# A hybrid decoder step: the sample's gated attention laid out by head and token, and rotary tables multiplied by their norm weights once per row

## The reference

```
A    = (q * exp(b)) (k * exp(-b))^T, kept where s <= t and the sample is the same
o    = (q * exp(b)) S + A v
S'   = exp(b_last) * S + (k * exp(b_last - b))^T v
out  = rms_norm(o) * weight * silu(r)
```

## Time and profile before

| | us |
|---|---|
| median of 3 runs | 5138.36 (5134.91 to 5141.19) |
| the profiled execution | 5144.09 |
| its span, first to last instruction | 5142.4 |
| granted TensorE clock, mean | 0.931 |
| stage of the sample's gated attention | 1398.3 to 1500.5 |
| stage of the prompt's attention | 1708.5 to about 2009 |

### The profile page before, as it was taken

The page is one execution under the profiler, slowest core; times in us unless marked ns, Lnnn a source line. Parts: engine busy times, 40 slices in busy tenths (PEclk is TensorE's granted clock), DMA queues, the critical chain, the costliest instruction groups (busy, mean ns, idle before and its releaser), DMA issues.

```text
span 5142.4 us, 56147 instructions
## 1 busy us (share of the span) xinstructions
PE 4326.8 (84%) x18857; PEld 2636.9 (51%) x18857; DVE 2540.6 (49%) x5464; ACT 1773.5 (34%) x4656; POOL 1531.9 (30%) x1445
## 2 busy tenths in 40 slices
PE   6999999985458467897988989889888898888997
PEld 5888888873345455343434434334444343443361
DVE  3111111126532494224666666666666666666645
ACT  3111111114302354212444444444444444444433
POOL 0000000004420591001443444444434444444423
PEclk9999999996659778898999999999999999999979
DMA  8798989762226674316999999999999999999979
GB/s 266 265 320 295 325 289 305 264 220 88 86 91 246 208 227 161 132 54 245 421 420 421 407 421 411 412 421 409 421 414 411 421 412 418 418 407 418 410 292 386
DMA packets 312463, 1626.90 MB, mean 316 GB/s; under 512 B 43176, under 2 KB 86280, under 8 KB 170296
## 3 DMA queue, kind: packets, MB, share of 16 engines
q0 software_dynamic: 164032, 1166.28, 55.4%
q1 hardware_dynamic: 112752, 236.06, 13.5%
q10 hardware_dynamic: 35456, 221.91, 13.0%
HBM read 1541.75 MB, written 311.61 MB: 360 GB/s over the span
## 4 chain that ended last, share of the span: by engine, by line
DMA 29%; PE 17%; ACT 4%; issue 3%; POOL 1%; DVE 0%; DVEq 0%; POOLq 0%; SPq 0%; ACTq 0%; PEldq 0%
DMA ex_rows<-scratch_uv,ex_E 29%; PE ex_ps_y L2451 13%; PE ex_ps_q L2420 3%; PE ex_ps_t L2383 1%; ACT ex_diag L2176 1%; ACT ex_w L2168 1%; POOL ex_rows L2113 1%; ACT L2164 1%; ACT L2159 1%; ACT ex_gel L2164 0%; ACT L2135 0%; ACT L2133 0%; PE ex_ps_s L2433 0%; DVE ex_dots L2317 0%; ACT ex_ex L2159 0%
## 5 line engine op out<-in xcount | busy, mean ns | idle before, releaser
L2451 PE MATMUL ex_ps_y<-ex_rows,ex_diag 128*128 128x512 f32 (+1 forms) x4224 | 2019.7, 613 | 315.8 <-ACT ex_diag L2176 293.9
L2317 DVE CUSTOM_DVE_ANT_0 ex_rows<-ex_rows,ex_n2u 128x1024 f32<-128x1024 f32 x1056 | 1294.6, 1226 | 943.6 <-DMA ex_rows<-scratch_uv,ex_E 925.2
L2113 POOL DMA_INDIRECT ex_rows<-scratch_uv,ex_E x1056 | 1135.8, 1076 | 1732.0 <-PE ex_ps_y L2451 1538.9
L2451 PEld LDWEIGHTS ex_ps_y<-ex_rows,ex_diag 128*128 128x128 f32 (+1 forms) x4224 | 747.4, 189 | 1479.8 <-ACT ex_diag L2176 747.3
L344 PE MATMUL pj_ps<-pj_w_hi,pj_nT 128*128 128x470 f32 x3072 | 699.3, 378 | 23.6 <-PE pj_ps L350 12.3
L2164 ACT ACTIVATE ex_gel<-ex_dots 128x1 f32<-128x1 f32 x1056 | 214.0, 203 | 1362.3 <-DVE ex_dots L2317 1361.2
L344 PEld LDWEIGHTS pj_ps<-pj_w_hi,pj_nT 128*128 128x128 f32 x3072 | 580.1, 189 | 109.1 <-issue 29.4
L2176 ACT ACTIVATE ex_diag<-ex_ident,ex_w 128x128 f32<-128x128 f32 x1024 | 411.1, 401 | 33.6
L248 DVE COPY pj_zo<-pj_ps 128x470 f32<-128x470 f32 x96 | 61.4, 646 | 725.9 <-PE pj_ps L344 502.8
L344 PE MATMUL pj_ps<-pj_w_lo,pj_nT 128*128 128x470 f32 x1536 | 361.5, 377 | 0.0
L248 ACT COPY pj_zo<-pj_ps 128x470 f32<-128x470 f32 x96 | 51.9, 552 | 830.1 <-PE pj_ps L344 469.3
(11 more groups left out here) (361 smaller groups left out, 3797.6 us busy)
## 6 DMA issues: line engine op xcount, KB each, us to landing
pj_w<-in_w_in POOLq DMA_DIRECT2D x24, 1880.0 KB, 34.3
scratch_z<-pj_zo SPq DMA_DIRECT2D x192, 235.0 KB, 11.1
scratch_uv<-in_peer_u ACTq DMA_DIRECT2D x8, 4096.0 KB, 25.8
scratch_uv<-in_peer_v ACTq DMA_DIRECT2D x8, 4096.0 KB, 43.2
scratch_uv<-in_peer_u ACTq DMA_DIRECT2D x4, 8192.0 KB, 42.5
scratch_uv<-in_peer_v ACTq DMA_DIRECT2D x4, 8192.0 KB, 73.3
out_dk_s<-in_cache_dil_k ACTq DMA_DIRECT2D x8, 4088.0 KB, 43.8
out_dv_s<-in_cache_dil_v ACTq DMA_DIRECT2D x8, 4088.0 KB, 55.9
```

The lines of the kernel that those rows point to most:

```text
L2113: pool.indirect_dma_start(out=rows[:, p % SLOTS, :], out_offset=None, in_=d["uv"], in_offset=bass.IndirectOffsetOnAxis(ap=E[:, turn % 4, k ...
L2317: nc.vector.tensor_tensor_reduce(out=row, in0=row, in1=n2u[:, tile % 2], scale=1.0, scalar=0.0, op0=ALU.mult, op1=ALU.add, accum_out=dots[ ...
L2451: last = nc.tensor.matmul(y[0:n, 512 * c:512 * c + 512], diag[:, p % DIAGS, 0:n], rows[:, p % SLOTS, D + 512 * c:D + 512 * c + 512], start ...
```

## The change

In `gla_sample`, head and token together (4 x 32) now stand on the partitions: `q`, `k`, `v`, `r` are loaded head by head into 32 partitions each. The output is made upright: for each sample and head one product with `own_q` (`qin` with the columns of all other samples zero) as weights and the state's 256 columns moving, the four heads into four quarters of the partitions of one bank. Added states use the quarter of the partitions that belongs to the head, and a bank per head. New states go into a second tensor `S2` and are stored one by one as they are made. `og` is stored from ScalarE's queue. `er` (the gate) gets the norm weight on GpSimd. At the end of the stage's programs SyncE loads the prompt's whole rotary table, and GpSimd multiplies it by the norm weights, 8 products, and stores the result (1024 rows x 2 KB) into the scratch tensor `n2`.

In `attend`, that result is loaded per turn (2 KB a row, two buffers) in place of the table (1 KB a row); the table product and the six broadcasts of weights are gone. The load for turn u waits for `t1` and `t2` of turn u-2.

```diff
 @block.sync   # gla_sample
-            sp.dma_start(qk[:], z[rows, C_Q:C_Q + 2 * H * DK].rearrange("t (h e) -> t h e", e=DK)).then_inc(z_in, 16)
...
+            for h in range(H):
+                sp.dma_start(q[heads[h]], z[rows, C_Q + h * DK:C_Q + (h + 1) * DK]).then_inc(qk_in, 16)
+                sp.dma_start(k[heads[h]], z[rows, C_K + h * DK:C_K + (h + 1) * DK]).then_inc(qk_in, 16)
+            for h in range(H):
+                sp.dma_start(v[heads[h]], z[rows, C_V + h * DV:C_V + (h + 1) * DV]).then_inc(v_in, 16)
+            for i in range(B):
+                sp.dma_start(S[:, i], d["state_gla"][i].rearrange("h p e -> p h e")).then_inc(S_in, 16)
+            sp.dma_start(tab[:], d["rope"][0:SEQ, :].rearrange("(n p) (c e) -> p n c e", p=P, c=2)).then_inc(tab_in, 16)
+            for n, g in enumerate((d["dil_qn_g"], d["dil_kn_g"])):
+                sp.dma_start(gain[:, 0, n, :], g.partition_broadcast(P)).then_inc(tab_in, 16)
...
-            sp.wait_ge(og_done, 1)
-            sp.dma_start(d["acts"][rows, 0:H * DV], og[:]).then_inc(stored, 16)
-            for q in range(B):
-                sp.wait_ge(S_done, q + 1)
-                sp.dma_start(d["gla_state_s"][q].rearrange("h p e -> p h e"), S[:, q]).then_inc(stored, 16)
+            for i in range(B):
+                sp.wait_ge(S_done, H * (i + 1))
+                sp.dma_start(d["gla_state_s"][i].rearrange("h p e -> p h e"), S2[:, i]).then_inc(stored, 16)
 @block.gpsimd
+            for h in range(H):
+                pool.dma_start(own_causal[heads[h]], d["own_causal"]).then_inc(consts_in, 16)
+                pool.dma_start(own[heads[h]], d["own"]).then_inc(consts_in, 16)
...
+            nc.gpsimd.tensor_tensor(er[:], er[:], gn[:], ALU.mult).then_inc(scaled, 1)
+            pool.wait_ge(tab_in, 16 * 7)
+            for n in range(NT):
+                nc.gpsimd.tensor_tensor(tg[:, n], tab[:, n].unsqueeze(2).to_broadcast([P, 2, 2, DK]), gain[:], ALU.mult).then_inc(tg_done, 1)
+            pool.wait_ge(tg_done, NT)
+            pool.dma_start(d["n2"][0:SEQ, 0:512].rearrange("(n p) x -> p n x", p=P), tg[:].rearrange("p n c q e -> p n (c q e)")).then_inc(tg_stored, 16)
+            pool.wait_ge(tg_stored, 16)
 @block.vector
+            for i in range(B):
+                own_tokens = slice(T * i, T * i + T)
+                last = nc.vector.tensor_copy(own_q[:, i, :, own_tokens], qin[:, :, own_tokens])
+            last.then_inc(ownq_done, 1)
...
+            nc.vector.tensor_tensor(own_k[:], kinT[:].unsqueeze(1).to_broadcast([P, B, DK]), own[:].unsqueeze(2).to_broadcast([P, B, DK]),
+                                    ALU.mult).then_inc(ownk_done, 1)
+            def new_state(i):
                 for h in range(H):
+                    dve.wait_ge(kv_done, H * i + h + 1)
+                    nc.vector.scalar_tensor_tensor(out=S2[:, i, h, :], in0=S[:, i, h, :], scalar=eb[:, h, T * i + T - 1:T * i + T],
+                                                   in1=ps_kv[:, h, 0:DV], op0=ALU.mult, op1=ALU.add).then_inc(S_done, 1)
+            dve.wait_ge(S_in, 16 * B)
+            for i in range(4):
+                new_state(i)
+            dve.wait_ge(rms_done, 1)
+            dve.wait_ge(scaled, 1)
+            nc.vector.scalar_tensor_tensor(out=og[:], in0=o_v, scalar=stat[:, 2:3], in1=er[:], op0=ALU.mult, op1=ALU.mult).then_inc(og_done, 1)
+            for i in range(4, B):
+                new_state(i)
 @block.tensor
+            def added_state(i):
+                for h in range(H):
+                    if i:
+                        pe.wait_ge(S_done, H * (i - 1) + h + 1)
+                    nc.tensor.matmul(ps_kv[:, h, 0:DV], own_k[heads[h], i, :], v[heads[h], :], start=True, stop=True).then_inc(kv_done, 1)
+            pe.wait_ge(ownk_done, 1)
+            added_state(0)
+            pe.wait_ge(A_done, 1)
+            pe.wait_ge(ownq_done, 1)
+            pe.wait_ge(S_in, 16 * B)
             for h in range(H):
+                nc.tensor.matmul(o_v[heads[h]], A[heads[h], :], v[heads[h], :], start=True, stop=False)
+            for i in range(B):
                 for h in range(H):
+                    last = nc.tensor.matmul(o_v[heads[h]], own_q[:, i, h, :], S[:, i, h, :], start=False, stop=(i == B - 1))
+            last.then_inc(o_done, 1)
+            for i in range(1, B):
+                added_state(i)
 @block.sync   # attend, load_x
                 if is_dil(u):
-                    after(sp, tg_done, u - 2)
-                    for p0, n, a in rows(d["rope"][0:SEQ, :], u):
-                        sp.dma_start(tab[p0:p0 + n, u % 2], a.rearrange("t (c e) -> t c e", c=2)).then_inc(tab_in[u % 2].sem, 16)
+                    after(sp, t1_done, u - 2)
+                    after(sp, t2_done, u - 2)
+                    for p0, n, a in rows(d["n2"][0:SEQ, 0:512], u):
+                        sp.dma_start(tg[p0:p0 + n, u % 2], a.rearrange("t (c q e) -> t c q e", c=2, q=2)).then_inc(tg_in[u % 2].sem, 16)
 @block.gpsimd
-            def angles(u):
-                after(pool, tab_in[u % 2], u)
-                after(pool, t1_done, u - 1)
-                after(pool, t2_done, u - 1)
-                nc.gpsimd.tensor_tensor(tg[:], tab[:, u % 2].unsqueeze(2).to_broadcast([P, 2, 2, P]), gain[:],
-                                        ALU.mult).then_inc(tg_done.sem, 1)
```

More of the change, by code:

```diff
@@ L837, in _ @@
[L837 to L844 removed]
+            sp.dma_start(a[:], z[rows, C_A:C_A + RANK]).then_inc(a_in, 16)
@@ L846, in _ @@
+            sp.wait_ge(stored, 16 * B)
         @block.gpsimd
         def _(pool):
[L848 to L851, removed]
+            pool.dma_start(ident[:], d["ident"]).then_inc(consts_in, 16)
+            pool.dma_start(wg2[:], d["gla_wg2"]).then_inc(consts_in, 16)
@@ L893, in _ @@
             nc.scalar.activation(er[:], er[:], ACT.Exp, scale=-1.0).then_inc(sig_done, 1)
[L894 to L899, removed]
-            for h in range(H):
[L901 to L906, removed]
+            act.wait_ge(o_done, 1)
+            act.wait_ge(set_up, 2)
+            nc.scalar.activation(sq[:], o_v, ACT.Square, accum_out=stat[:, 0:1]).then_inc(sq_done, 1)
+            act.wait_ge(sq_done, 1)
+            nc.scalar.activation(stat[:, 1:2], stat[:, 0:1], ACT.Ln, bias=eps[:], scale=1.0 / DV).then_inc(lnv_done, 1)
+            act.wait_ge(lnv_done, 1)
+            nc.scalar.activation(stat[:, 2:3], stat[:, 1:2], ACT.Exp, scale=-0.5).then_inc(rms_done, 1)
+            act.wait_ge(og_done, 1)
+            for h in range(H):
+                act.dma_start(d["acts"][rows, h * DV:(h + 1) * DV], og[heads[h]]).then_inc(v_in, 16)
+            act.wait_ge(v_in, 16 * (3 * H + 1))
         @block.vector
@@ L932, in _ @@
             dve.wait_ge(kinT_out, 1)
-            for q in range(B):
-                nc.vector.tensor_scalar(own_k[:, q], kinT[:], own[:, q:q + 1], None, ALU.mult).then_inc(ownk_done, 1)
-            dve.wait_ge(oT_done, 1)
-            for q in range(B):
-                dve.wait_ge(kv_done, q + 1)
-                for h in range(H):
-                    last = nc.vector.scalar_tensor_tensor(out=S[:, q, h, :], in0=S[:, q, h, :],
-                                                          scalar=eb[:, h, T * q + T - 1:T * q + T],
-                                                          in1=ps_kv[:, q % 2, h, :], op0=ALU.mult, op1=ALU.add)
-                last.then_inc(S_done, 1)
+            nc.vector.tensor_tensor(own_k[:], kinT[:].unsqueeze(1).to_broadcast([P, B, DK]), own[:].unsqueeze(2).to_broadcast([P, B, DK]),
+                                    ALU.mult).then_inc(ownk_done, 1)
@@ L1218, in _ @@
                         crossed(n - 1)
-                if at(n, 0) is not None and is_dil(n):
-                    angles(n)
         @block.scalar
```

143 lines of the change are left out of this document (57 added, 86 removed).

## The result

The changed kernel takes 5082.66 us (median of 4, 5080.31 to 5084.16) against 5139.77 (4 runs, 5134.91 to 5144.97): 57 us less, a ratio of 0.9888 with a 95% interval of 0.9871 to 0.9905. 5076 was forecast, within 5060 to 5098. Its profiled execution has a span of 5079.9 us, against 5142.4; the profiled executions are 62.5 us apart and not 57, since the one of the kernel before was 4.3 us above its median.

A forecast was written before the change was run, and what follows sets the result against it. Stages run one after another behind a barrier, so each changed stage's saving counts in full: 50 us from the sample's stage plus 12 from the attention, 5138.4 - 62 = 5076 us, range 5060 to 5098.

The forecast's parts named there:

- TensorE late by 1.4 us: Sample's stage, start: more small loads and constants issued first, so TensorE starts at 1410.3, 1.4 us late.
- Four quarters at once: Sample's stage: products on four quarters of the partitions run side by side, for output (31/4 us) and new states.
- the quarters' row: Profile row of the projection: 64 records of 118 columns, each to another quarter, start 25 ns apart, so four run at once.
- 7.7 us at the lower clock: Sample's stage, output products: 72 records, 31 us one after another, take 7.7 us; bounds 3.9 and 31.
- Next stage at 52 us: Sample's stage ends at 1450.5, 52 us long where it was 102: 50 us less, bounds 55 and 16.
- GpSimd's eight: Sample's stage: eight table products on GpSimd at 1.26 us each, 10.1 us, at the worst 18.6.
- The start of the attention: Attention, before the turns: six broadcasts leave SyncE's queue, 2.9 us less.
- A turn of 7.2 to 7.75: Attention: without the table product, one `y` to the next takes 7.2 to 7.75 us, where it took 8.20.
- The last eight turns: Attention: each transfer is two, SyncE issues 12 a turn at 0.6 us, so turns take 7.6 to 8.2 us.
- From that load on, the time runs by its landing: two intervals at each gain nothing: Attention, where weights stand ahead of `x` at four places: only 12 of 23 intervals gain 0.7 us, 8.4 us.
- `v` late: Attention: behind the moved wait `v` leaves at 7.7 us and not 2, landing at 11.7, where TensorE wants it at 10.2.
- rival 2: Attention: the late `v` eats the turns, which take 8.2 us, gain 3, time 5085; chance 0.18.

The follow-up runs named there:

- cols_serial: Changed kernel with all 32 output products of the states written into the first head's quarter; 5087.2 us, one run.
- rows_serial: Changed kernel with all four heads' added states read from the first head's quarter of the rows; 5081.3 us, one run.
- sample_only: Changed kernel's sample stage without the rotary tables, with the attention of the kernel before; 5084.2 us, ratio to before 0.9887.
- w_late_tg_last: Changed kernel with weights as 24 blocks beside the memory turns and the multiplied table's load behind the store of `y`; 5061.1 us, ratio to before 0.9841.
- tg_last: Changed kernel with the multiplied table's load and its wait for `t1`, `t2` moved behind the store of `y`; 5078.2 us, ratio to before 0.9877.

## Why the prediction was right, and where it was not

- *TensorE late by 1.4 us*: it was not late, 10.4 us after the stage's start and 10.6 before. The last constant was issued 2.8 us later in the stage than before, but landed 4.0 us after its issue and not 6.9: one state's load had been issued ahead of it, where there had been four.
- *Four quarters at once*: right for the columns, as the quarters' row had shown, and for the rows, where no row had shown it. Both were settled by taking them away. The stores made one by one have no such run: the timelines alone show 9.9 us from TensorE's last product to the next stage, where there had been 21.
- *7.7 us at the lower clock* for the output: 5.8, since the clock rose 2.3 us after its first product with a state. In *cols_serial* it rose at the same time, so it is not the overlap that raised it. In *rows_serial* it rose 4.7 us after that product, and the 64 records took 5.95 us and not 4.78. So part of this gain was luck.
- *Next stage at 52 us*: 50.1. GpSimd's eight took 9.86 us, against 10.1. VectorE's operations on a tile of SBUF and one of PSUM, beside the last six, did not disturb them: each took 1.26 to 1.28 us, with or without them. The Trainium skill (page "GPSIMD Engine Reference", Specifications) names contention for VectorE's instructions with two SBUF inputs or in a 2-port mode. These had one SBUF input, and the trace agrees: the eight started 1.23 us apart throughout. VectorE's last state came at 40.7 us and not at 44.5, but the transfers behind took up about half of that. The tables were judged to cost about 1 us behind the last state; sample_only shows 5.2, because the states' and the table's stores share full queues: the last state's store landed 8.2 us after its issue, and 3.1 in sample_only.
- *The start of the attention*: 6.0 and not 2.9. The term was too small, since the six broadcasts cost not only their issue but stood ahead of the last constant in transfer. That constant was issued 2.9 us sooner, as forecast, and landed 2.8 us after its issue and not 6.6; VectorE waited for it and began 12.8 us after the stage's start, now 6.0. Against sample_only, which has the broadcasts, the gain is 4.6.
- *A turn of 7.2 to 7.75*: 7.25 to 7.45 where nothing else is in the way. The loop of `y`, scaling and crossed product is the right one. The last eight turns, put at 7.6 to 8.2 for their doubled transfers, were 7.26 or 7.27 in four of the eight, and 7.27 to 7.63 in w_late_tg_last: that term was too large.
- *"From that load on, the time runs by its landing: two intervals at each gain nothing"*: this is the step that failed. The intervals with weights don't gain nothing, they lose 8 to 12 us in all, which is what the other turns gain. About 5 of that is the moved wait, which packs the table, `v` and the stores directly ahead of the weights and of `x` (59.8 to 61.3 us in the changed kernel's executions, 55.8 in tg_last); for the rest the cause stays open. So the 9.1 us forecast for the turns became +2.9, no change within the scatter of 4. tg_last gives back 6 to 9 of it; with the weights out of these turns too (w_late_tg_last) they are 36 shorter.
- *`v` late*: the mechanism of rival 2 was there, in single turns (7 and 10, in which TensorE stood 3.46 and 1.64 us for it) and not in all; in a calm stretch `v` landed in time.

The total was right to 7 us, in part by luck: the sample's stage came out 2 us better and the attention's start 3, which covered 5 of the 12 us by which the turns came out worse.

## What to carry to other kernels

A faster loop is worth only what its transfers let it keep: look at the turns in which large loads stand ahead of the loop's own, and price those first. Here 12 MB of prefetched weights in four pieces cost the turns more (27 to 29 us) than the removed operation was worth to them (19). Cutting them into 24 pieces and spreading these over 24 turns was worth 24 us by the ratios (27 by the medians), together with one line of order mended, of which the order alone was some 5. When a wait is moved in a queue, look at what now leaves in one burst behind it.

## What the runs showed of the hardware

- Products on different quarters of the rows, each with its own bank, run side by side: at the lower clock eight records took 1.24 us in four quarters and 3.75 in one (rows_serial). So do those on different quarters of the columns: at the upper clock a record alone came every 0.215 us (cols_serial), in four quarters every 0.054 (40 weight loads in 2.17 us in the changed kernel).
- GpSimd's small constants landed 2.1 to 3.3 us after their issue where no state's load of 512 KB had been issued ahead of them (eleven in the changed kernel). With one ahead it was 4.0 there and 3.8 in the kernel before, with two to four ahead 5.7, 6.1 and 6.9 in the kernel before, although the states are on another queue.
